# RWKV output step and right-hand sides: products sorted by the shape of the array tile, output halves alternating, one clearing product per bank half

## What is computed

```python
def step(s, inp):
    r_t, w_t, k_t, v_t, a_t, b_t = inp
    sa = jnp.einsum('bhvk,bhk->bhv', s, a_t)
    s = s * w_t[:, :, None, :] + sa[..., None] * b_t[:, :, None, :] + v_t[..., None] * k_t[:, :, None, :]
    return s, jnp.einsum('bhvk,bhk->bhv', s, r_t)
```

## Time and profile before

| | |
|---|---|
| runs, median of 3 | 1028.47 us (1026.59 to 1029.01) |
| profiled execution, span from first to last instruction | 1024.5 us |
| what runs have beyond that span (median less span) | 4.0 us |
| TensorE (PE) busy | 998.7 us, 97% of the span |
| VectorE (DVE), ScalarE (ACT), GpSimd (POOL) busy | 698.6, 546.2, 40.8 us |

### The profile page before, as it was taken

One profiled execution on the slowest core, in us unless ns is written; L12 is line 12 of the kernel. 1 busy time (PEld: TensorE's weight loads), 2 busy tenths in 40 slices (PEclk: granted clock), 3 DMA queues, 4 the chain that ended last, 5 costly groups with the idle time before them and its releaser, 6 DMA issues.

```text
span 1024.5 us, 20191 instructions
## 1 busy us (share of the span) xinstructions
PE 998.7 (97%) x8416; PEld 967.2 (94%) x8416; DVE 698.6 (68%) x863; ACT 546.2 (53%) x707; POOL 40.8 (4%) x26
## 2 busy tenths in 40 slices
PE   6999999999999999998999999999999999999998
PEld 5998898998999999998988999999999999999998
DVE  5678754653878888899894755556786867555553
ACT  5556556553675555465653544344486665444442
POOL 0034121000000000000000000000000000000000
PEclk9999999999999999999999999999999999999999
DMA  7643333333554655545333364565543234556451
GB/s 277 230 176 115 137 121 101 111 119 123 191 198 158 225 206 169 201 165 206 124 117 125 133 242 164 205 205 169 205 158 109 101 124 170 201 195 208 170 205 42
DMA packets 24832, 169.12 MB, mean 165 GB/s; under 512 B 2752, under 2 KB 3264, under 8 KB 4800
## 3 DMA queue, kind: packets, MB, share of 16 engines
q1 hardware_dynamic: 24192, 165.98, 46.3%
q10 hardware_dynamic: 576, 2.20, 0.6%
HBM read 167.12 MB, written 1.05 MB: 164 GB/s over the span
## 4 chain that ended last, share of the span: by engine, by line
PE 80%; DVE 13%; ACT 5%; issue 2%; DMA 0%; DVEq 0%; ACTq 0%
PE G L590 13%; PE G L591 13%; PE G L592 13%; PE D L590 8%; PE D L592 8%; PE D L591 8%; DVE wlo L1765 4%; PE M L590 2%; PE M L592 2%; PE M L591 2%; ACT whi L1248 2%; PE M L827 1%; PE D L841 1%; PE D L1149 1%; PE D L1176 1%
## 5 line engine op out<-in xcount | busy, mean ns | idle before, releaser
L1765 DVE TENSOR_TENSOR wlo<-raw,whi 128x2048 fp32r<-128x2048 f32 x155 | 354.1, 2290 | 122.5 <-ACT whi L1248 122.3
L590 PE MATMUL G<-xh,whi 128*128 128x256 f32 x1280 | 361.7, 283 | 4.2 <-DVE xl L1786 2.9
L592 PE MATMUL G<-xh,wlo 128*128 128x256 f32 x1280 | 355.0, 277 | 0.0
L591 PE MATMUL G<-xl,whi 128*128 128x256 f32 x1280 | 355.0, 277 | 0.0
L1248 ACT ACTIVATE whi<-raw 128x2048 fp32r<-128x2048 f32 x155 | 295.6, 1910 | 50.3 <-PE D L592 47.2
L590 PEld LDWEIGHTS G<-xh,whi 128*128 128x128 f32 x1280 | 241.1, 188 | 11.1 <-DVE wlo L1765 6.5
L591 PEld LDWEIGHTS G<-xl,whi 128*128 128x128 f32 x1280 | 240.6, 188 | 1.3 <-issue 1.2
L592 PEld LDWEIGHTS G<-xh,wlo 128*128 128x128 f32 x1280 | 240.7, 188 | 0.0
L590 PE MATMUL D<-hh,whi 128*128 128x256 f32 x672 | 185.8, 276 | 0.8 <-issue 0.8
L591 PE MATMUL D<-hl,whi 128*128 128x256 f32 x672 | 185.6, 276 | 0.0
L592 PE MATMUL D<-hh,wlo 128*128 128x256 f32 x672 | 185.6, 276 | 0.0
(11 more groups left out here) (385 smaller groups left out, 1432.2 us busy)
## 6 DMA issues: line engine op xcount, KB each, us to landing
raw<-wall_dram SPq DMA_DIRECT2D x155, 1024.0 KB, 4.9
x<-x_dram SPq DMA_DIRECT2D x4, 256.0 KB, 5.2
mem<-mem_dram ACTq DMA_DIRECT2D x1, 1024.0 KB, 4.7
out_dram<-x SPq DMA_DIRECT2D x4, 256.0 KB, 2.3
poolw<-pool_w_dram ACTq DMA_DIRECT2D x1, 768.0 KB, 6.3
cst<-cst_dram SPq DMA_DIRECT2D x1, 448.0 KB, 12.0
lora<-lora_dram SPq DMA_DIRECT2D x1, 256.0 KB, 11.5
sgw<-sg_w_dram SPq DMA_DIRECT2D x1, 256.0 KB, 12.2
```

What stands on the lines that cost most here:

```text
L590: mm(out, w_h, hi, start=start, stop=False, skip_group_check=skip)
L591: mm(out, w_h, lo, start=False, stop=False, skip_group_check=skip)
L592: return mm(out, w_l, hi, start=False, stop=stop, skip_group_check=skip)
L1765: signal(tt(wlo[:, pan.slot, 0:w], raw[:, pan.slot, 0:w], f32(whi[:, pan.slot, 0:w]), SUB), "w_lo")
```

## The change

Two functions on TensorE change, and nothing else.

`rw_rhs(ch)`: the four products of the values come first and the four with the state behind them, where they stood in turn. Only heads 0 and 1 clear their bank (`start=h < 2`). For chunk 0 the four products and their order stay as they are.

`rw_out`: the products were made head by head, five for each, and each head's five went to one half of the partitions. Now the 16 products of shape 128\*64 come first, in the order `uu` for half 0, `uu` for half 64, `vn` for half 0, `vn` for half 64, and then the four of shape 64\*64, again with the halves in turn. Only the first product of each half clears (`start=j == 0 and ch == 0`). The number of products is the same: 20 in `rw_out`, 8 in `rw_rhs(1)`.

```diff
--- before.py
+++ after.py
@@ -859,14 +859,14 @@
                 pe.wait_ge(S("rw_prod"), 8)
             else:
                 pe.wait_ge(S("rw_state"), 1)
+            outs = [M[h % 2][:, 0, (h // 2) * 64:(h // 2 + 1) * 64] for h in range(4)]
             for h in range(4):
+                ins = mm(outs[h], gm[:, 4 * ch + h, 2, :], vn[:, ch, h * 64:(h + 1) * 64],
+                         start=h < 2, stop=ch == 0, skip_group_check=True)
+            for h in range(4 if ch else 0):
                 j, o = h // 2, 64 * (h % 2)
-                out = M[h % 2][:, 0, j * 64:(j + 1) * 64]
-                ins = mm(out, gm[:, 4 * ch + h, 2, :], vn[:, ch, h * 64:(h + 1) * 64],
-                         start=True, stop=ch == 0)
-                if ch:
-                    ins = mm(out, ar[o:o + 64, 2 * j + ch, 0, :], st[o:o + 64, j, :],
-                             start=False, stop=True)
+                ins = mm(outs[h], ar[o:o + 64, 2 * j + ch, 0, :], st[o:o + 64, j, :],
+                         start=False, stop=True, skip_group_check=True)
             ins.then_inc(S("rw_rhs"), 1)
             freed["M0"] = freed["M1"] = ("rw_b0", 2 * ch + 2)
 
@@ -894,14 +894,20 @@
         def rw_out():
 
             pe.wait_ge(S("rw_uu"), 2)
-            for h in range(4):
-                j, o = h // 2, 64 * (h % 2)
+            for j in range(2):
                 for ch in range(2):
-                    out = DB[2][o:o + 64, j, ch * P:(ch + 1) * P]
-                    mm(out, uu[:, ch, h, :], gm[:, 4 * ch + h, 1, :], start=True, stop=False)
-                    ins = mm(out, vn[:, ch, h * 64:(h + 1) * 64], gm[:, 4 * ch + h, 3, :], start=False, stop=ch == 0)
-                    if ch:
-                        ins = mm(out, st[o:o + 64, j, :], ar[o:o + 64, 2 * j + ch, 1, :], start=False, stop=True)
+                    for o in (0, 64):
+                        h = 2 * j + o // 64
+                        mm(DB[2][o:o + 64, j, ch * P:(ch + 1) * P], uu[:, ch, h, :], gm[:, 4 * ch + h, 1, :],
+                           start=j == 0 and ch == 0, stop=False, skip_group_check=True)
+                    for o in (0, 64):
+                        h = 2 * j + o // 64
+                        mm(DB[2][o:o + 64, j, ch * P:(ch + 1) * P], vn[:, ch, h * 64:(h + 1) * 64], gm[:, 4 * ch + h, 3, :],
+                           start=False, stop=ch == 0, skip_group_check=True)
+            for j in range(2):
+                for o in (0, 64):
+                    ins = mm(DB[2][o:o + 64, j, P:2 * P], st[o:o + 64, j, :], ar[o:o + 64, 2 * j + 1, 1, :],
+                             start=False, stop=True, skip_group_check=True)
             ins.then_inc(S("rw_yp"), 1)
 
         def rw_gn1():
```

## The result

The changed kernel took 1022.24 us in the median of 20 runs (1019.71 to 1028.31), the kernel before 1028.28 us in as many. The ratio is 0.9949, 95% interval 0.9938 to 0.9961. That is faster by about 5.2 us, 0.5%.

A forecast was written before the change was run, and what follows sets the result against it. TensorE was taken as the bound, busy 998.7 of 1024.5 us. Gains of 3.0 (rw_out) and 1.3 us (rw_rhs(1)) leave a span of 1020.2, plus 4.0 gives 1024.2 us; own range 1023.0 to 1025.3, for all 1022.3 to 1027.2.

The forecast's parts named there:

- TensorE is the bound there: From 231 to 262 us TensorE is busy 30.96 of 31.00 us, so time saved there should shorten the total.
- range for all: Total time over the forecast and its rivals: 1022.3 us (no second clock stretch) up to 1027.2 us.
- rw_out 2.50 us, gain 3.0: rw_out falls from 5.50 us: 1.91 for the 128*64 block plus 0.59 for the 64*64 block; gain 2.15 to 3.0.
- rw_rhs(1) 1.63 us, gain 1.3: rw_rhs(1) falls from 2.91 us: 1.04 for the 128*128 block plus 0.59 for the 64*128 block; gain 0.85 to 1.3.
- Rival 1: rw_out's 64*64 block: row halves sharing a bank don't overlap, 1.01 or 1.44 us; total 1024.6 to 1025.0 us; chance 0.14.
- the rule behind it: Skill text on PSUM: row tiles write different banks and cannot access the same one simultaneously; rw_out's 64*64 products all write D2.
- Rival 2: Nothing overlaps anew, only shape changes are saved: rw_out 4.61 us, rw_rhs(1) 2.05 us, total 1026.7 us; chance 0.09.
- Rival 3: TensorE's clock, at 0.50 in stretches from 483.7 and 534.9 us, takes the time back: 1025.9 to 1027.6 us; chance 0.08.
- Rival 4: Slower: the clock falls in the changed stretch itself and stays down, for instance 1034 us; chance 0.05.
- The clearing flags at nothing: In rw_rhs and rw_out, fewer clearing products cost or save nothing, since clearing and adding products are equally long.
- The reason for the overlap: In sg_mix and rw_out, two neighbours writing different halves run side by side, 0.055 us a record and not 0.108.
- The 4.0 us around the span: Runs lie 4.0 us above the profiled span, added to the 1020.2 us span to give the forecast.

The follow-up runs named there:

- e1: New rw_out with the old rw_rhs, against the kernel before: ratio 0.998 (0.9933 to 1.0027), rw_out 2.48 us.
- e2: New rw_rhs with the old rw_out, against the kernel before: ratio 0.9991 (0.9957 to 1.0024), rw_rhs(1) 1.63 us.
- e3: Changed kernel, but rw_out's 128*64 products go head by head, four in a row for a half; one execution, rw_out 3.08 us.
- e6: Changed kernel, but rw_out's 128*64 products go eight in a row for one half, then eight for the other; one execution, rw_out 3.84 us.
- e4: The changed kernel run again, unaltered: ratio 0.9949 (0.9912 to 0.9986) against the kernel before; its profiled execution took 1027.32 us.
- e10: The changed kernel run once more, unaltered, for comparison with a pooling edit: ratio 0.9959 (0.9926 to 0.9992) against the kernel before.
- e9: Changed kernel, but each of the eight first products in rw_out clears, not only two; computes something else; one execution, rw_out 2.48 us.
- e7: Changed kernel with one of two 512-column scratch products removed in the last feed-forward loop: ratio 0.998 (0.994 to 1.002); profiled execution 1041.14 us.
- e5: Changed kernel, halves still alternating, but rw_out's 64*64 products put back between the heads; one execution, 1034.96 us, rw_out 2.78 us.

## Why the prediction was right, by its own steps

- **TensorE is the bound there, and the gain comes out of the end.** Shown: 4.28 us at L625, and three comparisons of the changed kernel at 0.9949, 0.9949 and 0.9959. 4.3 us is a ratio of 0.9958, inside all three intervals.
- **The total.** The measured median, 1022.24 us, lies under the forecast's own range (1023.0 to 1025.3) and 0.06 us under the range for all. The ratio applied to the 1028.47 us that the forecast started from gives 1023.2 us, inside both. The spread of 2.4 us came from three runs; the 20 runs of before here spread by 4.3 us, and 25 in e1's job by 11.6. A total of five or ten runs could have missed 4.3 us, as those of e1 and e2 did theirs. The parts were forecast far better than the total.
- **rw_out 2.50 us, gain 3.0.** Measured 2.48 and 3.02, and 3.00 by e1.
- **rw_rhs(1) 1.63 us, gain 1.3.** Measured 1.63 and 1.28, and 1.26 by e2.
- **Rival 1 and the rule behind it.** The prediction ties the rule on banks to its second rival; the case that the rule describes is the first, since it touches only the 64\*64 block. The four 64\*64 products all write `D2`, on other rows for other halves, and took 0.58 us where one after another would be 1.01. Row halves that write different partitions of one bank do run side by side here. The Trainium skill, TensorEngine Tiling (Array Packing), "Gotcha 1: PSUM Pressure", says they cannot; by the measurement that doesn't hold for such a pair. For row halves that write the same partitions of a bank no run here shows it.
- **Rival 2**, only the shape changes are saved: 4.61 us in rw_out, against 2.48.
- **Rival 3, the clock.** It moved, and in the kernel's favour. After has 6.8 us at the lower level (from 480.4 and from 504.2 us, 3.4 each) and not 10.2. It varies from one execution to the next: 10.2 us before the end in e1 and e3, 3.4 in e6. In the runs it leans one way, though: the mean granted clock was 0.9956 in e4 and 0.9954 in e10, against 0.9938 and 0.9941 for the kernel before in the same jobs. On 1027 us that is an estimated 1.4 to 1.9 us less lost. The prediction had this only as the other side of a rival (1.7 us more, 1022.5 us), which came nearer to the measured 1022.24 us than the forecast did. No experiment moved the clock alone, so its part is argued and not shown. **Rival 4** didn't come: 231 to 262 us stayed at 1.00.
- **The clearing flags at nothing.** e9 agrees.
- **The reason for the overlap was too narrow.** The prediction put the overlap down to neighbours that write different halves, and the lack of it in the earlier trace rows to four in a row for one half. e3 shows that four in a row overlap in part as well, if no other shape stands between: what kept the halves apart before was the 64\*64 product. The forecast was not touched by that, since the change does both.
- **The 4.0 us around the span was mis-sized.** After shows 1.8 us (1026.81 less 1025.0), and every run that has both on record 1.75 to 1.95. Before's 4.0 was the median of runs against the span of one fast execution. It cancelled, since the 4.3 us were in effect taken from the median: 1028.28 less 4.3 is 1024.0 us. The medians differ by 6.0 us and the ratio says 5.2. What is beyond 4.3 was not settled. The clock's estimated 1.4 to 1.9 us are enough for it, and so is the chance of a wide loop (some 6 us each).

## What to carry to other kernels

When small products fill only half the rows or columns of the array, look at the order by tile shape first: here each change of shape cost 0.145 us and also ended all overlap between halves. Group by shape, and inside a group let the halves take turns; with four or eight in a row for one half only two products overlapped at each change of half. Judge such an edit by the distance between two instructions of the same stream in the trace, not by the total, when the total swings by more than the edit is worth.

## What was not expected of the hardware

The same float32r products in the same loop, at a granted clock of 1.00 and without a wait, run at one of two spacings, 0.113 or 0.1175 us, and keep it for 1400 products (885 or 851 in 100 us). The last loop costs 6.3 us more in the wide one. In the profiles of this study that were of the changed kernel itself (after, e4, e10), one of three loops was wide each time, and not always the same one. Less the wide loop's share (6.3 us, in e4 6.8 us for a loop of 1506 products) their spans are 1018.7, 1018.6 and 1019.1 us, against 1024.5 of before, which has no wide loop. A single product of 512 columns switches it: every narrow stream that met one went on wide, in e7 for the rest of the loop. The runs of the kernel before spread from 1025.59 to 1037.2 us in one job. That is the size of one or two wide loops, but no profile of a long run of that kernel was taken, so this is an inference; among the changed ones e5, with two wide loops, took 1034.96 us, and e7, with three, 1041.14.
